# Recurrent mixer of a four-layer block: second head group prepared inside the first group's levels

## The chip, the cores and the metric

One core of a Trainium2 chip runs the whole program. The metric is the device time of one execution in microseconds, here the median of the runs shown.

## The reference, cut to what matters

The program computes four transformer layers on 256 tokens of width 1024 in float32. Each layer is a SwiGLU feed-forward part, a mixer and another feed-forward part, each with an adaptive norm before it. The mixer of the first layer is the recurrent one:

```python
q, fz, i, g = jnp.split(h @ w_in, 4, axis=-1)
q = jax.nn.silu(q)
f = jax.nn.sigmoid(fz)          # lb is zero here: one such layer
logf, k = jnp.log(f), 1.0 - f
b = jnp.cumsum(lf_c, axis=2)    # inside a chunk of 64 tokens, per head and channel
att = einsum('bhtk,bhsk,bhtsk->bhts', q_c, k_c, exp(b_t - b_s) where s <= t)
new_state = exp(b_last) * state + einsum(k_c * exp(b_last - b), v_c)
o = rmsnorm(inter + intra, onorm_g) * jax.nn.silu(g)
return o @ w_out
```

There are 8 heads of 128 channels.

## The kernel before, in words

**Pieces.** Every weight matrix goes through the engines in pieces of 128 x 2048 floats (1 MB). SyncE loads a piece into one of three slots of `raw` with two transfers (L335 to 343), after the piece three before it has been split. ScalarE copies it, rounded, to `wH` (`cut`, L491 to 496), VectorE subtracts to get the rest, `wL` (`cut`, L806 to 810), and TensorE multiplies with three products (high by high, low by high, high by low). The copies have three slots as well: ScalarE's `cut` of a piece waits until TensorE has "eaten" the piece three before it (`s_eaten`). All engines have their own program, in a fixed order written out by hand, and meet only through semaphores.

**The mixer's input projection** has 16 pieces, two for each 512 columns of `a_w_in`. Numbered from 0 in the order before: v first half (0, 1), forget of head group 0 (2, 3), query of group 0 (4, 5), v second half (6, 7), g first half (8, 9), g second half (10, 11), forget of group 1 (12, 13), query of group 1 (14, 15). The output projection `a_w_out` has pieces 16 to 19. v and g are laid out by token (`by_token`, L1519, TensorE's L1399, L1401, L1403), forget and query by channel (`by_channel`, L1533, lines L1543, L1545, L1546). They land in the PSUM halves `GUf` and `PAf`; the halves `PBf` and `TMf` take the gram products.

**A head group** is four heads. Its preparation: ScalarE takes a sigmoid and an absolute value of the forget columns (L613, L614), VectorE a minimum (L1022); ScalarE a sigmoid of the query (L618), VectorE the product (L1026); ScalarE the softplus by exp and ln (L622, L623), VectorE a subtraction and a scan over the tokens (L1032, L1033). Then nine levels, n = 0 to 8. In level n VectorE writes the exponents of level n + 1 (`exponents`, L979 to 989), ScalarE takes the exponential (L632), VectorE multiplies q and k in (`decayed`, L997, L998), TensorE makes 8 gram products (L1579; the last level 4, L1581), and VectorE selects that level's part of them into the table `att` (`select`, L1005, L1008, L1010). Behind the last level TensorE multiplies the table with v (12 products, L1598 to 1601), ScalarE squares (L584), VectorE sums and normalizes (L956, L961), multiplies with the norm's weights and with g (L1050, L1053), TensorE turns the heads (L1612), ScalarE writes the high part of the result (L602) and VectorE the low part (L967).

**Order before.** Group 0's levels run with one projection piece in each of levels 0 to 7, pieces 8 to 15. Then the output norm of group 0, its turn and low part, then group 1's preparation, then group 1's levels, with the cuts of pieces 16 and 17 near their end. The projections of pieces 16 and 17 (they need group 0 alone) run while VectorE normalizes group 1; then the turn of group 1, cuts of 18 and 19, and their projections. The next phase is a feed-forward part. Its first pieces come through the same ring, and pieces of the adaptive weights go through the buffer `ada` of two slots (`load_ada`, L378 to 384).

Of the kernel before, what the change touches and what calls it, by code (L numbers as in the profile page):

```python
# [22 lines left out]
ALU = mybir.AluOpType  # L23
# [78 lines left out]
def build(nc, T, out, upto=99):  # L102

    with ExitStack() as ctx:
# [56 lines left out]
        k_, q_, b_ = (M[:, n * D:(n + 1) * D] for n in range(3))  # L161
        E = [M[:, n * D:(n + 1) * D] for n in (3, 4, 5)]
        att = M[:, 6 * D:7 * D].rearrange("p (h s) -> p h s", s=P)
        attX = M[:, 7 * D:7 * D + 512].rearrange("p (h s) -> p h s", s=P)
# [167 lines left out]
        def _(sp):  # L332
# [63 lines left out]
            def ffn(l, j):  # L396
# [91 lines left out]
        def _(act):  # L488
# [115 lines left out]
            def hgrn():  # L604
# [5 lines left out]
                for grp in range(2):  # L610
                    forget, query = (GUf, PAf) if grp else (PAf, GUf)
                    act.wait_ge(s_eaten, t.next("done", 2))
                    act.activation(k_, forget, ACT.Sigmoid, scale=-1.0)  # L613
                    act.activation(E[0], forget, ACT.Abs).then_inc(s_key, 1)  # L614
                    if grp == 0:
                        cut()
                    act.wait_ge(s_eaten, t.next("done", 2))
                    act.activation(E[1], query, ACT.Sigmoid).then_inc(s_sigq, 1)  # L618
                    if grp == 0:
                        cut()  # L620
                    act.wait_ge(s_key, t.next(s_key))
                    chained(act.activation(E[0], E[0], ACT.Exp, scale=-1.0))  # L622
                    act.activation(E[0], E[0], ACT.Ln, bias=1.0).then_inc(s_ln, 1)  # L623
                    if grp == 0:
# [3 lines left out]
                    for n in range(9):  # L628
                        if n < 8:
                            act.wait_ge(s_expo, t.next(s_expo))  # L630
                            e = E[(n + 1) % 3]
                            act.activation(e, e, ACT.Exp).then_inc(s_decay, 1)  # L632
                        if grp == 0 and n < 6 or grp == 1 and n in (6, 8):
                            cut()
                        if grp == 0 and n == 3:
                            evacuate(g_[:, :, 0:512], GU[:, :, :], ACT.Silu)
                        if grp == 0 and n == 5:
                            evacuate(g_[:, :, 512:D], PY[:, 0:2, :], ACT.Silu)
                    head_norm(TMf, E[0])
                    head_root(8)  # L640
                    high_out(xH[:, 4 * grp:4 * grp + 4, :].rearrange("p d s -> p (d s)"), GUf if grp else PBf)
                cut()
                cut()
# [154 lines left out]
        def _(dve):  # L798
# [170 lines left out]
            def exponents(n, e):  # L969
# [3 lines left out]
                if n < 8:  # L973
                    m = 1 << (n - 1)
                    b4, e4 = (a.rearrange("p (g two m) -> p g two m", two=2, m=m) for a in (b_, e))
# [8 lines left out]
                b4, e4 = (a.rearrange("p (h c m) -> p h c m", h=4, c=4) for a in (b_, e))  # L984
# [7 lines left out]
            def decayed(n, e):  # L992
# [3 lines left out]
                e4, q4, k4 = (a.rearrange("p (g two m) -> p g two m", two=2, m=m) for a in (e, q_, k_))  # L996
# [3 lines left out]
            def select(n):  # L1000
# [3 lines left out]
                if n == 0:  # L1004
                    ins = dve.tensor_tensor(att, src, bc(ident.unsqueeze(1), [P, 8, P]), ALU.mult)  # L1005
                elif n < 8:
                    mask = cst[:, C_LEVEL + (n - 1) * P:C_LEVEL + n * P].bitcast(I32)
                    ins = dve.copy_predicated(att, bc(mask.unsqueeze(1), [P, 8, P]), src)  # L1008
                else:
                    ins = dve.tensor_copy(attX, src[:, 0:4, :])  # L1010
# [3 lines left out]
            def hgrn():  # L1014
# [4 lines left out]
                for grp in range(2):  # L1019
                    forget, query = (GUf, PAf) if grp else (PAf, GUf)  # L1020
                    dve.wait_ge(s_key, t.next(s_key))
                    dve.tensor_scalar(b_, forget, 0.0, None, ALU.min).then_inc(s_readD, 1)  # L1022
                    if grp == 0:
                        cut()
                    dve.wait_ge(s_sigq, t.next(s_sigq))
                    dve.tensor_tensor(q_, E[1], query, ALU.mult).then_inc(s_readD, 1)  # L1026
                    dve.wait_ge(s_readD, t.next(s_readD, 2))
                    if grp == 0:
                        cut()

                    dve.wait_ge(s_ln, t.next(s_ln))
                    chained(dve.tensor_tensor(E[1], b_, E[0], ALU.subtract))  # L1032
                    chained(dve.tensor_tensor_scan(b_, cst[:, C_SCAN:C_SCAN + 4 * S], E[1], 0.0, ALU.mult, ALU.add))  # L1033
                    if grp == 0:
                        cut()
                        cut()
                    for n in range(9):
                        if n < 8:
                            exponents(n + 1, E[(n + 1) % 3])
                        if n:  # L1040
                            decayed(n, E[n % 3])
                            select(n - 1)
# [878 lines left out]
```

## Time and profile before

| what | value |
|---|---|
| three runs | 2619.49, 2624.07, 2625.35 us; median 2624.07 |
| span of the profiled execution | 2623.9 us (its own time is not listed apart from the span) |
| TensorE matmuls busy | 2425.2 us, 92% |
| VectorE busy | 1732.2 us, 66% |
| ScalarE busy | 1097.4 us, 42% |
| recurrent mixer in the span | about 297 to 495 us |

Times in the views are microseconds from the span's start. PE is TensorE, DVE is VectorE, ACT is ScalarE, SPq is SyncE's queue. In the windows a row gives for each engine busy time and number of instructions, and behind them the granted TensorE clock (1.00 is full), the share of the DMA engines and GB/s. In the timeline a row ends with the idle time before the instruction and what released it. In the chain a row is a start, a length and what the end of the program hung on in that time.

### The profile page before, as it was taken

To read this page: it belongs to the slowest core of one execution; us is meant where nothing else is said; L and a number is where in the kernel's file an instruction comes from. 1 tells how busy PE (TensorE), PEld (TensorE's weight loads), DVE (VectorE), ACT (ScalarE), POOL (GpSimd) and SP (SyncE) were. 2 spreads that over 40 slices of the span, in tenths; PEclk is the share of its full clock that TensorE was granted. 3 is DMA by queue.
4 is the path that set the end of the run, shared out by engine and by line. 5 is a ranking of instruction groups with operands and counts; after the bars stand their busy time and mean duration, and the time that the engine had idled before them with its cause. 6 is when DMAs were issued, how large, how long until landed. Compare 5 with 4: busy or idle time off the path is not lost.

```text
span 2623.9 us, 32924 instructions
## 1 busy us (share of the span) xinstructions
PE 2425.2 (92%) x11906; PEld 2043.9 (78%) x11906; DVE 1732.2 (66%) x2090; ACT 1097.4 (42%) x1220; POOL 0.2 (0%) x4
## 2 busy tenths in 40 slices
PE   8999994899999995999999898999999989899998
PEld 8788884788788773788788796778878878777886
DVE  4777576687587785677687644568757764455444
ACT  1443543434433454433534334544343333463443
POOL 0000000000000000000000000000000000000000
PEclk9999997999999995999999987999999998898999
DMA  9788440498588640498498832248858892324553
GB/s 336 253 302 274 152 137 8 138 319 265 193 296 293 217 164 29 147 314 271 164 320 294 228 117 85 97 160 301 275 193 282 294 277 94 113 81 129 176 185 111
DMA packets 349089, 530.28 MB, mean 202 GB/s; under 512 B 14833, under 2 KB 208465, under 8 KB 348881
## 3 DMA queue, kind: packets, MB, share of 16 engines
q1 hardware_dynamic: 349008, 529.18, 60.6%
q8 instruction: 54, 0.88, 0.1%
q14 instruction: 27, 0.21, 0.0%
HBM read 528.08 MB, written 1.05 MB: 202 GB/s over the span
## 4 chain that ended last, share of the span: by engine, by line
PE 78%; DVE 12%; ACT 5%; issue 2%; SPq 2%; DMA 1%; DVEq 0%; ACTq 0%
PE GU L1399 12%; PE GU L1403 12%; PE GU L1401 12%; PE PY L1399 9%; PE PY L1401 9%; PE PY L1403 8%; DVE wL L810 3%; ACT wH L496 2%; PE TM L1473 2%; PE PY L1417 2%; PE GU L1485 2%; DVE acc L839 1%; PE TM L1449 1%; PE PY L1729 1%; PE PY L1627 1%
## 5 line engine op out<-in xcount | busy, mean ns | idle before, releaser
L810 DVE TENSOR_TENSOR wL<-raw,wH 128x2048 fp32r<-128x2048 f32 x352 | 794.5, 2279 | 308.7 <-ACT wH L496 308.0
L496 ACT ACTIVATE wH<-raw 128x2048 fp32r<-128x2048 f32 x352 | 659.5, 1899 | 223.1 <-PE PY L1403 101.4
L1399 PE MATMUL GU<-wH,xH 128*128 128x512 f32 (+1 forms) x1600 | 634.4, 397 | 28.3 <-issue 11.6
L1403 PE MATMUL GU<-wH,xL 128*128 128x512 f32 (+1 forms) x1600 | 623.2, 390 | 0.0
L1401 PE MATMUL GU<-wL,xH 128*128 128x512 f32 (+1 forms) x1600 | 622.5, 389 | 0.0
L1399 PEld LDWEIGHTS GU<-wH,xH 128*128 128x128 f32 x1600 | 302.5, 189 | 93.6 <-issue 29.4
L554 ACT ACTIVATE hH<-TM 128x512 fp32r<-128x512 f32 x88 | 52.6, 598 | 747.1 <-PE TM L1449 747.1
L839 DVE SCALAR_TENSOR_TENSOR acc<-ada,cs,acc 128x512 f32<-128x512 f32 x448 | 336.9, 752 | 23.1 <-DVE acc L839 2.6
L1403 PEld LDWEIGHTS GU<-wH,xL 128*128 128x128 f32 x1600 | 301.9, 189 | 63.5
L1401 PEld LDWEIGHTS GU<-wL,xH 128*128 128x128 f32 x1600 | 302.5, 189 | 58.3
L1399 PE MATMUL PY<-wH,hH 128*128 128x512 f32 x704 | 226.7, 403 | 26.2 <-DVE hL L920 24.8
L1401 PE MATMUL PY<-wL,hH 128*128 128x512 f32 x704 | 220.2, 394 | 0.0
L1403 PE MATMUL PY<-wH,hL 128*128 128x512 f32 x704 | 218.4, 392 | 0.0
L920 DVE TENSOR_TENSOR hL<-TM,hH 128x512 fp32r<-128x512 f32 x88 | 60.9, 692 | 234.7 <-ACT hH L554 231.2
L1399 PE MATMUL PY<-wH,xH 128*128 128x512 f32 x432 | 177.4, 411 | 8.3 <-DVE wL L810 6.9
L1401 PE MATMUL PY<-wL,xH 128*128 128x512 f32 x432 | 173.3, 401 | 0.0
L1403 PE MATMUL PY<-wH,xL 128*128 128x512 f32 x432 | 173.0, 401 | 0.0
L1399 PEld LDWEIGHTS PY<-wH,hH 128*128 128x128 f32 x704 | 128.1, 190 | 50.9 <-DVE wL L810 18.2
L1401 PEld LDWEIGHTS PY<-wL,hH 128*128 128x128 f32 x704 | 133.2, 189 | 30.0
L1403 PEld LDWEIGHTS PY<-wH,hL 128*128 128x128 f32 x704 | 133.3, 189 | 29.7
L1399 PEld LDWEIGHTS PY<-wH,xH 128*128 128x128 f32 x432 | 85.0, 197 | 30.3 <-issue 8.6
L550 ACT ACTIVATE sh<-GU 128x512 f32<-128x512 f32 x88 | 52.7, 598 | 118.2 <-PE GU L1403 118.2
(295 smaller groups left out, 2324.5 us busy)
## 6 DMA issues: line engine op xcount, KB each, us to landing
ada<-in_ada_w SPq DMA_DIRECT2D x128, 1024.0 KB, 7.5
raw<-in_ffn_wi SPq DMA_DIRECT2D x176, 512.0 KB, 6.0
raw<-in_ffn_w_in SPq DMA_DIRECT2D x176, 512.0 KB, 5.6
raw<-in_ffn_wo SPq DMA_DIRECT2D x88, 512.0 KB, 4.4
raw<-in_ffn_w_out SPq DMA_DIRECT2D x88, 512.0 KB, 4.4
raw<-in_mix_w_in SPq DMA_DIRECT2D x64, 512.0 KB, 4.8
M<-in_ada_w SPq DMA_DIRECT2D x16, 1024.0 KB, 8.5
raw<-in_a_w_in SPq DMA_DIRECT2D x32, 512.0 KB, 4.7
```

Source lines behind the costliest of these rows:

```text
L496: act.activation(wH[:, slot, 0:words], raw[:, slot, 0:words], ACT.Copy).then_inc(s_high, 1)
L550: act.activation(sh[:, 0, :, :], GU[:, :, 0:CF], ACT.Silu).then_inc(s_silu, 1)
L554: act.activation(hH[:, :, :].rearrange("p f s -> p (f s)"), TM[:, 0, :], ACT.Copy).then_inc(s_hh, 1)
L810: dve.tensor_tensor(wL[:, slot, 0:words], raw[:, slot, 0:words], wH[:, slot, 0:words], ALU.subtract).then_inc(s_split, 1)
L839: ins = dve.scalar_tensor_tensor(acc[:, :], w, c, acc[:, :], ALU.mult, ALU.add)
L920: dve.tensor_tensor(hL[:, :, :].rearrange("p f s -> p (f s)"), TM[:, 0, :], hH[:, :, :].rearrange("p f s -> p (f s)"), ALU.subtract).then_ ...
L1399: pe.matmul(outs[i], aH, wh[i], start=first, stop=False)
L1401: pe.matmul(outs[i], aH, wl[i], start=False, stop=False)
L1403: ins = pe.matmul(outs[i], aL, wh[i], start=False, stop=last)
L1417: ins = pe.matmul(PT[:, i, d, :], x[:, i, d * P:(d + 1) * P], diag[:, i, :], start=True, stop=True)
L1473: ins = pe.matmul(bank[:, k:k + 1], acc[:, k * P:(k + 1) * P], ones[:, :], start=fresh, stop=True, skip_group_check=not fresh)
L1485: ins = pe.matmul(GU[:, c % 2, n:n + 1], w, cs[:, 4 * q + k:4 * q + k + 1], start=(q == 0 and k == tiles[0] and n == 0), stop=False, skip_ ...
```

## The change

The group 1 tables `k_`, `q_`, `b_` and the log of the forget gate get places of their own in the buffer `ada`, which is free during the mixer, and `att`, `attX` of group 1 in `xn`. With this group 1 can be prepared while group 0's levels run. Norm scratch moves from `E[0]` to `shf`. Every `decayed`, `exponents`, `select` is the same instruction as before.

- The pieces are loaded in another order: v first half (0, 1), forget 0 (2, 3), query 0 (4, 5), forget 1 (6, 7), query 1 (8, 9), g first half (10, 11), v second half (12, 13), g second half (14, 15), then `a_w_out` (16 to 19).
- TensorE multiplies pieces 6 and 7 ahead of the levels, 8 and 9 in levels 0 and 1 of group 0, 10 and 11 in its levels 3 and 4; 12 and 13 in levels 0 and 1 of group 1, 14 and 15 in its levels 3 and 4. Output products of group 0 go to `GU`, directly ahead of gram 0 of group 1. Group 0's heads are turned in level 5 of group 1.
- ScalarE and VectorE do group 1's forget in level 1 of group 0, its query, softplus and scan in level 3. Cuts are made in levels 0, 1, 2, 3, 4 and 5 of group 0 and in 0, 1, 4 and 5 of group 1. The norm of group 0 is in level 1 of group 1, its high and low part in level 6. Piece 19 is cut behind the norm of group 1.
- SyncE waits, in the next feed-forward part, for the second turn of heads before it loads adaptive weights into `ada`.

The core of the diff:

```diff
+                        if with_ada and (l, j) == (0, 2):
+                            sp.wait_ge(s_ot, 2)
                         if with_ada:
                             load_ada(la, c0 + i, 0)
...
-                    for lo in (2 * D, D, 0, 2 * D + 512, 3 * D, 3 * D + 512, D + 512, 512):
+                    for lo in (2 * D, D, 0, D + 512, 512, 3 * D, 2 * D + 512, 3 * D + 512):
...
+                # ScalarE
+                forget(0, E[0])
+                cut()
+                query(E[1])
+                cut()
+                softplus(E[0])
+                cut()
+                for n in range(8):
+                    decay(n)
+                    if n < 3:
+                        cut()
+                    if n == 1:
+                        forget(1, lf_[1])
+                    if n == 3:
+                        query(q_[1])
+                        softplus(lf_[1])
+                        cut()
+                    if n == 4:
+                        cut()
+                    if n == 5:
+                        evacuate(g_[:, :, 0:512], PY[:, 0:2, :], ACT.Silu)
+                        cut()
+                for n in range(8):
+                    decay(n)
+                    if n == 0:
+                        cut()
+                    if n == 1:
+                        head_norm(GUf, shf)
+                        head_root(8)
                         cut()
                         evacuate(v_[:, :, 512:D], PY[:, 0:2, :])
...
+                    if n == 4:
+                        cut()
+                    if n == 5:
+                        evacuate(g_[:, :, 512:D], PY[:, 0:2, :], ACT.Silu)
+                        cut()
+                    if n == 6:
+                        high_out(xH[:, 0:4, :].rearrange("p d s -> p (d s)"), GUf)
+                head_norm(TMf, shf)
+                head_root(8)
+                cut()
+                high_out(xH[:, 4:8, :].rearrange("p d s -> p (d s)"), GUf)
...
+                # VectorE
+                forget(0)
+                cut()
+                query(0, E[1])
+                cut()
+                log_decay(0, E[0], E[1])
+                cut()
+                for n in range(9):
+                    level(0, n)
+                    if n < 3:
+                        cut()
+                    if n == 1:
+                        forget(1)
+                    if n == 3:
+                        query(1, q_[1])
+                        log_decay(1, lf_[1], lf_[1])
+                        cut()
+                    if n == 4 or n == 5:
+                        cut()
+                select(0, 8)
+                for n in range(9):
+                    level(1, n)
+                    if n == 0:
+                        cut()
+                    if n == 1:
+                        normed(0, GUf)
+                        cut()
+                    if n == 4 or n == 5:
+                        cut()
+                    if n == 6:
+                        low(0)
+                select(1, 8)
+                normed(1, TMf)
+                cut()
+                low(1)
...
+                # TensorE
+                by_channel(PAf, 0)
+                by_channel(PAf, 1)
...
+                pe.wait_ge(s_readD, t.next(s_readD))
+                for n in range(9):
+                    gram(0, n)
+                    if n < 2:
+                        by_channel(GUf, n)
+                    if n == 3:
+                        pe.wait_ge(s_readD, t.next(s_readD))
+                        by_token(B, 0)
+                    if n == 4:
+                        by_token(B, 1)
+                pe.wait_ge(s_readD, t.next(s_readD))
+                outputs(0, GU)
+                for n in range(9):
+                    gram(1, n)
+                    if n == 0 or n == 3:
+                        pe.wait_ge(s_readA, t.next(s_readA))
+                        by_token(B, 0)
+                    if n == 1 or n == 4:
+                        by_token(B, 1)
+                    if n == 5:
+                        turn_heads(0)
+                outputs(1, TM)
+                pe.wait_ge(s_readA, t.next(s_readA))
+                pe.wait_ge(s_xl, t.next(s_xl))
+                project(0, 0)
+                project(0, 1)
+                turn_heads(1)
                 pe.wait_ge(s_xl, t.next(s_xl))
                 project(1, 0)
                 project(1, 1)
```

Here `level(grp, n)` is `exponents` of n + 1, `decayed` of n and `select` of n - 1, and `log_decay` is the subtraction and the scan.

## Rows read from the trace of the kernel before

**Rows 1.** The page: its head and the busy times.

```profile
span 2623.9 us, 32924 instructions
PE 2425.2 (92%) x11906; PEld 2043.9 (78%) x11906; DVE 1732.2 (66%) x2090; ACT 1097.4 (42%) x1220; POOL 0.2 (0%) x4
```

**Rows 2.** The windows by stages of the mixer.

```profile
331.00:398.00 67.00, 60.91 (x413) 56.53 (x412) 47.84 (x51) 29.14 (x23) 0.00 (x0) 0.95 0.38 126
...
398.00:426.00 28.00, 10.08 (x61) 9.00 (x59) 13.35 (x13) 13.64 (x13) 0.00 (x0) 0.65 0.00 1
...
426.00:460.00 34.00, 18.11 (x121) 16.49 (x121) 32.73 (x45) 12.06 (x10) 0.00 (x0) 0.85 0.08 24
```

**Rows 3.** The chain of waits: gram products inside group 0's levels.

```profile
344.42 3.79 PE TM L1579 x16
...
353.87 1.78 PE PY L1579 x16
...
361.12 1.79 PE TM L1579 x16
```

**Rows 4.** VectorE's timeline: cuts, norm, low part, scan, ends of group 1's levels.

```profile
331.04 4.49 DVE L810 TENSOR_TENSOR wL<-raw,wH 128x2048 fp32r<-128x2048 f32 x2
...
399.49 0.69 DVE L1010 COPY M<-PY 128x512 f32<-128x512 f32 x1 [5.38 <-PE PY L1581]
404.35 1.22 DVE L956 TENSOR_REDUCE st<-M 128x8 f32<-128x1024 f32 x1 [4.16 <-ACT M L584]
...
408.80 1.22 DVE L1053 TENSOR_TENSOR M<-M 128x1024 f32<-128x1024 f32 x1
413.14 1.23 DVE L967 TENSOR_TENSOR xL<-PY,xH 128x1024 fp32r<-128x1024 f32 x1 [3.12 <-ACT xH L602]
...
423.37 2.29 DVE L1033 TENSOR_TENSOR_SCAN M<-cst,M 128x1024 f32<-128x1024 f32 x1
425.69 0.69 DVE L979 TENSOR_TENSOR M<-M 128x512 f32<-128x512 f32 x1
...
453.78 2.29 DVE L810 TENSOR_TENSOR wL<-raw,wH 128x2048 fp32r<-128x2048 f32 x1
...
459.20 0.69 DVE L1010 COPY M<-PY 128x512 f32<-128x512 f32 x1 [0.72 <-PE PY L1581]
```

**Rows 5.** ScalarE's timeline: a cut, then table loads and softplus of group 0.

```profile
320.76 1.91 ACT L496 ACTIVATE wH<-raw 128x2048 fp32r<-128x2048 f32 x1
322.69 1.28 ACT L622 ACT_TABLE_LOAD   x1
...
326.36 1.06 ACT L623 ACTIVATE M<-M 128x1024 f32<-128x1024 f32 x1
```

**Rows 6.** The windows: granted clock around TensorE's idle stretches.

```profile
342.00:344.00 2.00, 0.00 (x0) 0.00 (x0) 2.00 (x4) 0.81 (x1) 0.00 (x0) 0.50 0.44 71
...
404.00:408.00 4.00, 0.00 (x0) 0.00 (x0) 3.28 (x5) 1.74 (x3) 0.00 (x0) 0.81 0.00 0
...
434.00:438.00 4.00, 2.31 (x21) 2.12 (x20) 3.96 (x6) 1.06 (x1) 0.00 (x0) 1.00 0.00 0
...
460.00:464.00 4.00, 4.00 (x19) 4.00 (x20) 2.22 (x1) 0.00 (x0) 0.00 (x0) 0.50 0.26 86
```

**Rows 7.** The chain of waits: group 0's outputs done, then group 1's, to the next phase.

```profile
403.22 1.03 ACT M L584
...
459.95 0.80 PE TM L1598 x2
...
475.98 0.89 PE GU L1612 x8
...
482.18 0.77 PE PY L1399
...
489.33 1.93 ACT wH L496
```

**Rows 8.** The page: the mixer's weight loads, size and time to landing.

```profile
raw<-in_a_w_in SPq DMA_DIRECT2D x32, 512.0 KB, 4.7
```

More of the change, by code:

```diff
@@ L609, in hgrn, with forget @@
                 cut()
-                for grp in range(2):
-                    forget, query = (GUf, PAf) if grp else (PAf, GUf)
+                def forget(grp, e):
                     act.wait_ge(s_eaten, t.next("done", 2))
-                    act.activation(k_, forget, ACT.Sigmoid, scale=-1.0)
-                    act.activation(E[0], forget, ACT.Abs).then_inc(s_key, 1)
-                    if grp == 0:
-                        cut()
-                    act.wait_ge(s_eaten, t.next("done", 2))
-                    act.activation(E[1], query, ACT.Sigmoid).then_inc(s_sigq, 1)
-                    if grp == 0:
+                    act.activation(k_[grp], PAf, ACT.Sigmoid, scale=-1.0)
+                    act.activation(e, PAf, ACT.Abs).then_inc(s_key, 1)
@@ new lines, in query, with softplus, decay @@
+                def query(e):
+                    act.wait_ge(s_eaten, t.next("done", 2))
+                    act.activation(e, GUf, ACT.Sigmoid).then_inc(s_sigq, 1)
+                def softplus(e):
+                    act.wait_ge(s_key, t.next(s_key))
+                    chained(act.activation(e, e, ACT.Exp, scale=-1.0))
+                    act.activation(e, e, ACT.Ln, bias=1.0).then_inc(s_ln, 1)
+                def decay(n):
+                    act.wait_ge(s_expo, t.next(s_expo))
+                    e = E[(n + 1) % 3]
+                    act.activation(e, e, ACT.Exp).then_inc(s_decay, 1)
@@ L626, in hgrn @@
                         cut()
                         evacuate(v_[:, :, 512:D], PY[:, 0:2, :])
[L628 to L638, printed above, removed]
@@ L967, in low_out, with exponents @@
                 dve.tensor_tensor(dst, src, high, ALU.subtract).then_inc(s_xl, 1)
-            def exponents(n, e):
+            def exponents(grp, n, e):
                 if n < 8:
                     m = 1 << (n - 1)
-                    b4, e4 = (a.rearrange("p (g two m) -> p g two m", two=2, m=m) for a in (b_, e))
+                    b4, e4 = (a.rearrange("p (g two m) -> p g two m", two=2, m=m) for a in (b_[grp], e))
                     shape = [P, 4 * S // (2 * m), m]
@@ L983, in exponents @@
                     return
[L984 removed]
+                b4, e4 = (a.rearrange("p (h c m) -> p h c m", h=4, c=4) for a in (b_[grp], e))
                 chained(dve.tensor_tensor(e4[:, :, 0:2, :], bc(b4[:, :, 0:2, 63:64], [P, 4, 2, 64]), b4[:, :, 0:2, :],
@@ L1018, in hgrn, with forget, query @@
                 cut()
-                for grp in range(2):
-                    forget, query = (GUf, PAf) if grp else (PAf, GUf)
+                def forget(grp):
                     dve.wait_ge(s_key, t.next(s_key))
-                    dve.tensor_scalar(b_, forget, 0.0, None, ALU.min).then_inc(s_readD, 1)
-                    if grp == 0:
-                        cut()
+                    dve.tensor_scalar(b_[grp], PAf, 0.0, None, ALU.min).then_inc(s_readD, 1)
+                def query(grp, e):
@@ L1033, in hgrn @@
[L1033 to L1042, printed above, removed]
-                        if grp == 0 and n < 6 or grp == 1 and n == 7:
-                            cut()
@@ L1555, in hgrn @@
                 norm_and_first()
-                A, B = [GU[:, i, :] for i in range(NT)], [PY[:, i, :] for i in range(NT)]
+                B = [PY[:, i, :] for i in range(NT)]
                 by_channel(PAf, 0)
@@ new lines, in hgrn, with gram @@
+                by_channel(PAf, 0)
+                by_channel(PAf, 1)
+                def gram(grp, n):
+                    if n:
+                        pe.wait_ge(s_z, t.next(s_z))
+                    if n > 1:
+                        pe.wait_ge(s_sel, t.next(s_sel))
+                    dst = (PBf if n % 2 == 0 else TMf).rearrange("p (h s) -> p h s", s=P)
+                    e = E[n % 3].rearrange("p (h s) -> p h s", s=P)
+                    kk, qq = (e, e) if n else (a[grp].rearrange("p (h s) -> p h s", s=P) for a in (k_, q_))
+                    for h in range(8 if n < 8 else 4):
+                        if n < 8:
+                            ins = pe.matmul(dst[:, h, :], kk[:, h, :], qq[:, h, :], start=True, stop=True)
+                        else:
+                            ins = pe.matmul(dst[:, h, :], kk[:, 2 * h, :], qq[:, 2 * h + 1, :], start=True, stop=True)
+                    ins.then_inc(s_gram, 1)
@@ L1595, in hgrn, with outputs @@
+                def outputs(grp, banks):
                     pe.wait_ge(s_sel, t.next(s_sel, 2))
```

109 lines of the change are left out of this document (35 added, 74 removed).

## The prediction

> **What bounds the kernel now.** The page comes first: TensorE works over 92% of the span, VectorE over 66% [rows 1]. These shares mix four layers; the change touches only the recurrent mixer, from about 297 to 495 us. So the second view is the windows by its stages [rows 2]. The reader is to see three regimes. From 331 to 398 (levels of head group 0) TensorE works 61 of 67 us. From 398 to 426 (tail of group 0, preparation of group 1) no engine works more than half the time. From 426 to 460 (levels of group 1) VectorE works 32.7 of 34 us. The third view, the chain of waits, confirms it: a group 0 level takes 7.24 us (353.87 to 361.12) on TensorE, 1.79 of gram products and 5.45 of a by-token piece [rows 3]; the nine levels of group 1 take 34.2 us of VectorE with one cut among them (425.69 to 459.89) [rows 4].
>
> **The change, part by part.** No arithmetic is added or taken: the same pieces, products and passes. Three things move. (a) Projection pieces: group 1's forget and query pieces come forward, v's second half and both g halves go back; group 0's levels then carry four pieces and not eight, group 1's four and not none. (b) Group 1's forget, query, softplus and scan run inside levels 1 and 3 of group 0. (c) Group 0's output norm and its low part run inside levels 1 and 6 of group 1. So the hole between the last gram selection of group 0 (ends 400.2) and the first exponents of group 1 (425.69) goes: 25.5 us [rows 4].
>
> What takes its place, by VectorE's in-order queue, from 331.04, where the first scan ends. Work: the levels of one group are 31.0 us (425.69 to 459.89, less the 2.29 of a cut and 0.9 of waits), twice 62.0; eleven cuts of about 2.25, 24.8; forget, query and subtraction of group 1, each one pass over 1024 floats like the low part of 1.23, and the scan of 2.29, together 6.0; norm of group 0 from 404.35 to 410.02, 5.7, and a low part of 1.23 [rows 4]. Sum 99.7, which would end group 1 at 430.7 and not 459.9, 29 us earlier. That holds only if VectorE never waits. The waits, each found by laying the new order out with the durations of the rows:
>
> In group 0: 2.9 us before the second cut of its levels (exponential, then ScalarE's cut of 1.91, now one behind the other) [rows 5]. Two sigmoid passes, each behind a table load of 1.28, leave about 1.0 each. Softplus of group 1 takes ScalarE 4.73 us (322.69 to 327.42) [rows 5], of which 1.2 lies beside the query product: 3.5. In level 5, ScalarE is told to wait for g's first half (Silu) before it cuts: the piece behind gram 4 starts only when VectorE has done the exponents of level 4 behind softplus and scan, about 372.4, and with grams at the low clock 3.4 and the piece 6.0 it is eaten at 382; Silu 1.03 and cut 1.91 follow, so VectorE, ready at 380.1, waits 4.8. Some 0.8 for late grams. Sum 14, so group 0 ends at about 399, one us before today. Group 0 carries less TensorE work but no less time: its cover is gone to VectorE's queue.
>
> In group 1: the cut of piece 15 (g, second half of the rows) sits right behind exponents of level 0. It may be written only when piece 12 (v, second half) is eaten, since the ring has three slots, and TensorE eats piece 12 only after the twelve output products of group 0 and gram 0 of group 1: 3.0 (400.2 to 403.22 now) + 1.8 + 5.45, from 399.1 to 409.4 [rows 3, 7]. ScalarE's cut ends at 411.3; VectorE was ready at 400.2 and stands 11 us. Behind the standing instruction are all of level 1, and with it gram 1, and with gram 1 the next piece. So the same wait comes back smaller: cut of piece 16 waits for piece 13 (eaten about 425.5; VectorE ready at 423.0 after the norm): 4.5. Piece 17 waits for 14: 4.6. Piece 18 waits for 15, with Silu ahead: 2.8. Sum 23. Group 1 ends at about 430.7 + 14 + 23 = 468, 8 us later than now.
>
> The tail. Now: from 459.95 to 475.98 run the outputs and two projection pieces, which at 5.45 each leave 5.1 for the outputs at the low clock; then the turn 0.9, then high part 1.02, the cut of piece 18 (1.91 and 2.29), and the third projection piece, from 482.18, half of it at the low clock, is eaten at 489.3 [rows 7]: 29.3 in all, and from there the next phase starts through a cut. After: piece 18 is cut long before, so the cut goes out of the path and low part (1.23) comes in: 5.1 + 10.9 + 0.9 + 1.1 + 1.3 + 5.45 = 24.8, with 0.3 of hops 25.1. This gives back 4.2. The wait added to SyncE's queue before the next phase's adaptive weights (until the second turn of heads, about 485) costs nothing: today the next pieces of the ring come ahead of it in the queue and the cut before the next phase is at 489.33 [rows 7]; it is issued about then, with the next pieces behind it in the queue not earlier either. The mixer's own loads are the same 32 transfers in another order; each is issued when the piece three before it is split and lands in 4.7 us [rows 8], over 7 us before its cut is due in the new order: nothing. Group 1's tables lie in other buffers, in passes of the same shape: nothing either.
>
> **Sum**: 8.2 − 4.2 = +4. The nearest bounds: TensorE at full clock through the outputs gives 2.1 back (3.0 for 5.1); at the low clock through every late block it costs more (rival 1). The tail's third piece may or may not meet the low clock, 1.4. I take +3.5, as one of the two may fall well: 2623.9 + 3.5 = 2627.4. The span and the median of the runs shown (2624.07) differ by 0.2, so the sum stands for both. What a measurement of this kernel can tell from no change is about 0.2%, 5 us.
>
> A rule that bears on the sum stands in the clock. The rows: TensorE's granted clock stood at 0.50 in 342 to 344, while it waited for VectorE, and a gram from 344.42 ran slow; it fell again within 404 to 408 with TensorE idle, was 1.00 at 434 to 438 and 0.50 through the outputs at 460 to 464 [rows 3, 6]. A gram at 0.50 (1.2 GHz) takes 3.79 and not 1.79 [rows 3]. The sum takes the low level where TensorE stood over 5 us before a block, and full clock for outputs and piece 12.
>
> The Trainium skill ("TensorE: Matmul & The Clock Gate", HAM oscillation) says that idle gaps between bursts put TensorE back to half rate and that each new burst then starts cold; it advises to keep the work contiguous. By that rule this change, which breaks eight contiguous pieces into short bursts, is worse than my sum: rival 1, priced below from the rows.
>
> **Rivals.**
> 1. *Low clock at every late block: slower.* TensorE waits 3 to 7 us before nearly every gram of the new order. Where the next VectorE wait hangs on the block (outputs with piece 12, pieces 14 and 15, the third projection piece), a cold start costs 2.1, 2.2, 2.2 and 1.4 (a block of gram and piece was 9.45 cold, 344.42 to 353.87, against 7.24) [rows 3]: +7.9 on the forecast, so 2635.3. For it: the outputs of 460 to 464, cold behind sparse grams. Against: at 434 to 438 the same sparse grams ran at 1.00 [rows 6].
> 2. *The wait at the group boundary does not bite: faster.* If piece 12 were eaten by the time VectorE comes to cut 15, 11 us go and 2627.4 becomes 2616.4. It decides at whether waits of VectorE from 331 to the end of group 1 sum to under 33 (29 less work time plus 4 of tail); I have 37. For it: 25.5 us of hole do go, and my waits are a layout. Against: the piece stands behind the outputs in TensorE's order, and the cut ahead of level 1 in both other queues.
> 3. *It moves work and no time: none.* Group 0 is paced by VectorE as long as it was by TensorE, and group 1 stretches by as much as the hole held: 0, 2624. It is where the forecast goes if two or three small waits fall away; near it, only the mechanism is the same.
>
> **Chances.** Forecast 0.50 (its own range 2622 to 2633), rival 1 0.22, rival 2 0.16, rival 3 0.12. Slower by over 0.2% is all of rival 1 and a third of the forecast: 0.38. Faster by over 0.2%: rival 2 and a little: 0.17. Within: 0.45. The range leaves out the outer parts of rivals 1 and 2: 2615 to 2638.
>
> **What would show it.** Right: no hole between group 0's last selection and group 1's first exponents; group 1's levels take near 68 us, VectorE's longest wait is on ScalarE's cut right after its first exponents, about 11 us, with ScalarE waiting on TensorE's by-token piece; group 0's levels still end near 399; the third projection piece starts 2 to 3 us after the turn, with no cut before it. Each of the 4 us waits should be found on a cut in levels 1, 4 and 5. Wrong: VectorE busy over 85% from 400 to 460 (rival 2), or granted clock under 0.7 over the group 1 levels (rival 1).

## The result and the profile after

| | before | after |
|---|---|---|
| median, 20 runs each | 2623.84 us | 2631.31 us |
| lowest to highest | 2619.49 to 2627.72 | 2623.61 to 2633.86 |
| ratio, with its 95% interval | | 1.0023 [1.0017, 1.0029] |
| span of the profiled execution | 2623.9 us | 2627.2 us |
| mixer, from one norm's gate copy to the next | 218.8 us | 224.6 us |

The change makes the program about 6 us slower (0.23% of 2624; the two medians of 20 runs differ by 7.5), where +3.5 with the range 2615 to 2638 was forecast. The last row is read from ScalarE's copies of the gate (292.45 and 511.25 before, 293.00 and 517.56 after), which enclose the mixer's part of the trace. It shows +5.8 us. That the spans differ by only 3.3 comes from the later phases, in which nothing is changed; so the mixer's row is the one that the runs agree with. The gate copy stands behind the next norm, so that stretch takes in a little of the next phase too.

The head of the page after the change:

```profile
span 2627.2 us, 32931 instructions
PE 2429.1 (92%) x11906; PEld 2048.5 (78%) x11906; DVE 1732.4 (66%) x2090; ACT 1101.0 (42%) x1223; POOL 0.2 (0%) x4
```

The work is the same [rows 1]: as many matmuls, as many VectorE instructions, three more on ScalarE (table loads). So all of the time is in waits and in the clock. The same stages by windows, 332 to 399 for the levels of group 0 and 399 to 472 for those of group 1 (which were 426 to 460 before [rows 2]):

```profile
332.00:399.00 67.00, 47.60 (x279) 43.42 (x277) 51.55 (x54) 35.67 (x28) 0.00 (x0) 0.82 0.32 110
...
399.00:472.00 73.00, 50.76 (x264) 44.95 (x264) 46.29 (x55) 25.12 (x21) 0.00 (x0) 0.79 0.18 58
```

The columns are those of [rows 2]: the third number from the end is the granted clock. VectorE works 46.3 of 73 us in group 1's levels, where it was at 32.7 of 34 before. TensorE no longer fills group 0's levels (47.6 of 67 and not 60.9), and those take as long as before. The hole of 25.5 us is gone, and its time is back in small pieces. VectorE's timeline shows them, with the wait at the end of the row [rows 4]:

```profile
385.78 2.29 DVE L840 TENSOR_TENSOR wL<-raw,wH 128x2048 fp32r<-128x2048 f32 x1 [4.92 <-ACT wH L499]
...
398.47 0.69 DVE L1040 COPY M<-PY 128x512 f32<-128x512 f32 x1
399.20 0.69 DVE L1009 TENSOR_TENSOR M<-ada 128x512 f32<-128x512 f32 x1
399.81 0.69 DVE L1012 TENSOR_TENSOR M<-ada 128x512 f32<-128x512 f32 x1
411.54 2.29 DVE L840 TENSOR_TENSOR wL<-raw,wH 128x2048 fp32r<-128x2048 f32 x1 [11.04 <-ACT wH L499]
...
428.55 2.29 DVE L840 TENSOR_TENSOR wL<-raw,wH 128x2048 fp32r<-128x2048 f32 x1 [5.46 <-ACT wH L499]
...
447.61 2.29 DVE L840 TENSOR_TENSOR wL<-raw,wH 128x2048 fp32r<-128x2048 f32 x1 [5.37 <-ACT wH L499]
...
456.44 2.29 DVE L840 TENSOR_TENSOR wL<-raw,wH 128x2048 fp32r<-128x2048 f32 x1 [2.89 <-ACT wH L499]
...
470.12 1.33 DVE L1038 COPY_PREDICATED xn<-cst,TM 128x1024 f32<-128x1024 int32 x1 [1.12 <-PE TM L1636]
```

Group 1 begins 0.04 us behind the last selection of group 0 (399.16 to 399.20). Then VectorE stands 11.04 us before the cut of piece 15, and before each of the three cuts behind it. ScalarE's timeline tells what it stood for:

```profile
400.53 1.06 ACT L631 ACTIVATE M<-M 128x1024 f32<-128x1024 f32 x1 [6.03 <-DVE M L1012]
409.60 1.91 ACT L499 ACTIVATE wH<-raw 128x2048 fp32r<-128x2048 f32 x1 [8.01 <-PE PY L1463]
...
426.60 1.91 ACT L499 ACTIVATE wH<-raw 128x2048 fp32r<-128x2048 f32 x1 [7.52 <-PE PY L1463]
```

The exponential ends at 401.6, the cut may start only at 409.6: until then TensorE makes the outputs, gram 0 of group 1 and piece 12. That is the ring of three slots: the copy of piece 15 goes where piece 12 still lies.

### The profile page after: what moved, and what is told of

Same layout as the page of the kernel before. It is cut to its first block, busy times and chain, and to the rows that moved or that the text cites. A ratio compares the mean times of both kernels' runs of the same rounds, so it can differ in the third digit from the quotient of the medians.

```text
span 2627.2 us, 32931 instructions
## 1 busy us (share of the span) xinstructions
PE 2429.1 (92%) x11906; PEld 2048.5 (78%) x11906; DVE 1732.4 (66%) x2090; ACT 1101.0 (42%) x1223; POOL 0.2 (0%) x4
## 4 chain that ended last, share of the span: by engine, by line
PE 77%; DVE 12%; ACT 6%; issue 3%; DMA 1%; SPq 1%; DVEq 0%; ACTq 0%
PE GU L1459 12%; PE GU L1463 12%; PE GU L1461 12%; PE PY L1459 9%; PE PY L1461 9%; PE PY L1463 9%; DVE wL L840 3%; ACT wH L499 3%; PE TM L1533 2%; PE GU L1545 2%; DVE acc L869 1%; PE PY L1477 1%; PE TM L1509 1%; PE PY L1802 1%; PE PY L1700 1%
## 5 line engine op out<-in xcount | busy, mean ns | idle before, releaser
L1459 PE MATMUL GU<-wH,xH 128*128 128x512 f32 (+1 forms) x1584 | 628.0, 396 | 28.9 <-issue 11.6
L1459 PE MATMUL PY<-wH,hH 128*128 128x512 f32 x704 | 226.6, 403 | 25.3 <-DVE hL L950 23.9
L950 DVE TENSOR_TENSOR hL<-TM,hH 128x512 fp32r<-128x512 f32 x88 | 60.9, 692 | 236.9 <-ACT hH L557 234.0
L1459 PE MATMUL PY<-wH,xH 128*128 128x512 f32 x448 | 184.5, 412 | 5.3 <-DVE xL L997 2.4
L1461 PE MATMUL PY<-wL,xH 128*128 128x512 f32 x448 | 180.1, 402 | 0.0
L1463 PE MATMUL PY<-wH,xL 128*128 128x512 f32 x448 | 179.3, 400 | 0.0
L1463 PEld LDWEIGHTS PY<-wH,xL 128*128 128x128 f32 x448 | 87.5, 195 | 19.4
```

Source lines behind the costliest of these rows:

```text
L950: dve.tensor_tensor(hL[:, :, :].rearrange("p f s -> p (f s)"), TM[:, 0, :], hH[:, :, :].rearrange("p f s -> p (f s)"), ALU.subtract).then_ ...
L1459: pe.matmul(outs[i], aH, wh[i], start=first, stop=False)
L1461: pe.matmul(outs[i], aH, wl[i], start=False, stop=False)
L1463: ins = pe.matmul(outs[i], aL, wh[i], start=False, stop=last)
```

## The experiments

Each kernel was timed against the kernel before on the same chip. "Mixer" is again the stretch between the two gate copies of its profile: 218.8 us before, 224.6 with the change. "To the end of group 1" is its part up to VectorE's last selection: 167.4 us before. What is left is the tail and the next norm.

| run | ratio to before | interval | to the end of group 1, us | mixer, us |
|---|---|---|---|---|
| the change | 1.0023 | 1.0017 to 1.0029 | 179.2 | 224.6 |
| cut 15 later | 0.9968 | 0.9955 to 0.998 | 166.6 | 211.0 |
| piece 12 early | 0.998 | 0.9971 to 0.999 | 172.3 | 217.7 |
| scan at the boundary | 1.0014 | 1.0005 to 1.0023 | 178.8 | 226.6 |
| group 0 laid out anew | 0.9976 | 0.9967 to 0.9985 | 165.1 | 212.8 |
| filler in the tail | 1.0015 | 1.0006 to 1.0024 | 178.5 | 222.3 |
| fillers in group 1 | 1.0015 | 1.0006 to 1.0024 | 176.0 | 221.4 |
| both groups anew | 0.9914 | 0.9902 to 0.9927 | 147.4 | 192.8 |
| the same and filler | 0.99 | 0.9887 to 0.9914 | 147.3 | 191.1 |
| the same, two cuts ahead | 0.9886 | 0.9871 to 0.9901 | 142.4 | 186.8 |

The two columns of microseconds come from one profiled execution each, and part of a mixer's length is not the edit's doing. Where nothing was edited, the stretch from the last cut before the next norm to the gate copy took 18.7 us with the change, 19.4 in the run with cut 15 later and 21.1 in two others, by where TensorE met the low clock in it (granted 0.50 from 509 to 512.6 in one of the two, 1.00 with the change); and the end of group 0 came 105.6 to 106.4 us behind the gate copy in four kernels that are the same up to there. So a difference of 1 us between two profiles tells little, and one of 2 us only where it is found at the edited place.

### The wait at the group boundary

ScalarE, and VectorE likewise:

```diff
                 for n in range(8):
                     decay(n)
-                    if n == 0:
-                        cut()
                     if n == 1:
                         head_norm(GUf, shf)
                         head_root(8)
                         cut()
+                    if n == 2:
                         evacuate(v_[:, :, 512:D], PY[:, 0:2, :])
+                        cut()
```

> The changed kernel with the cut of piece 15 moved from level 0 of group 1 to behind the norm of group 0 in level 1, and the cut of piece 16 to level 2. Ring theory (the cut at the group boundary makes VectorE stand until TensorE has eaten piece 12, 11.0 us in the changed kernel's trace): VectorE starts level 1 at once and does the norm in that time; the cut of 15 finds its slot free, the cut of 16 waits 2 to 3 us for piece 13. Laid out with the durations of the trace, the cut of 16 ends near 422 and not 430.8 with level 2 behind it and not ahead, so group 1 ends 12 us earlier: ratio to before about 1.0023 - 0.0046 = 0.998, 2618 us. Low-clock theory (the time goes into TensorE's cold starts, VectorE's stand is only where it shows): moving a cut leaves the gaps of TensorE as they are, so little goes: under 3 us, ratio about 1.001 to 1.002.

(On ScalarE the copy of v's second half moves along, out of level 1 into level 2.) Measured: 0.9968, 13.6 us off the mixer, 12.6 of them by the end of group 1, where 12 were expected. The part between the groups, by VectorE's timeline of that run:

```profile
397.29 0.69 DVE L1040 COPY M<-PY 128x512 f32<-128x512 f32 x1
...
402.87 1.23 DVE L1035 TENSOR_TENSOR xn<-PY,cst 128x1024 f32<-128x1024 f32 x1 [1.13 <-PE PY L1636]
...
410.35 2.29 DVE L840 TENSOR_TENSOR wL<-raw,wH 128x2048 fp32r<-128x2048 f32 x1 [0.54 <-ACT wH L499]
...
418.52 2.29 DVE L840 TENSOR_TENSOR wL<-raw,wH 128x2048 fp32r<-128x2048 f32 x1 [2.20 <-ACT wH L499]
...
434.69 2.29 DVE L840 TENSOR_TENSOR wL<-raw,wH 128x2048 fp32r<-128x2048 f32 x1 [6.25 <-ACT wH L499]
```

The 11.04 us are down to 0.54, because level 1 and the norm now lie ahead of the cut. The cut of piece 16 waits 2.20, as expected; that of piece 17 waits 6.25 for 5.37. Two cuts moved in two queues turn the slower kernel into one 0.3% faster than before. The low-clock theory allowed 3 us and falls as the main cause. This run alone would not quite settle it, since with TensorE at work all through 399 to 412 its clock stayed up behind:

```profile
412.00:420.00 8.00, 5.34 (x32) 4.56 (x30) 5.80 (x7) 3.88 (x3) 0.00 (x0) 1.00 0.39 131
```

With the change it was 0.50 there. What the clock is worth by itself the fillers in group 1 show below: 3.2 us.

The condition of the prediction's faster rival was tried by itself: TensorE multiplies piece 12 in level 5 of group 0.

```diff
                     if n == 4:
                         by_token(B, 1)
+                    if n == 5:
+                        pe.wait_ge(s_readA, t.next(s_readA))
+                        by_token(B, 0)
...
-                    if n == 0 or n == 3:
+                    if n == 3:
```

> The changed kernel with TensorE's product of piece 12 moved from behind the outputs of group 0 (level 0 of group 1) into level 5 of group 0, where TensorE idles; cuts stay. This is the condition of the prediction's faster rival: piece 12 eaten before VectorE comes to cut 15. Ring theory: the 11.0 us wait shrinks to the 3 us that ScalarE's cut takes behind the exponential; piece 13 is eaten near 415.5 and cut 16 ends at about 420 and not 430.8: 11 us earlier, ratio 0.998 to 0.999, about 2619 us. If the prediction's price for the rival is wrong because the waits behind it grow instead (each later cut waits for the piece three before it, and those hang on VectorE, not on piece 12), the gain is under 5 us: ratio about 1.0005 or more. Low-clock theory: the extra work in level 5 keeps the clock up for the grams of levels 6 to 8, a gain of 1 to 2 us there in addition.

Measured: 0.998, which against 1.0023 is the 11 us expected. Its one profile shows less: the mixer is only 6.9 us shorter. That profile is of the slowest of the nine runs (2625.77 us, median 2621.24), so the two need not agree. The wait at the boundary went from 11.04 to 2.92, which is 8.1; the end of group 0 came 1.2 later, with a wait of 1.20 for a gram behind the added piece. The wait behind the boundary stayed:

```profile
404.79 2.29 DVE L840 TENSOR_TENSOR wL<-raw,wH 128x2048 fp32r<-128x2048 f32 x1 [2.92 <-ACT wH L499]
...
421.82 2.29 DVE L840 TENSOR_TENSOR wL<-raw,wH 128x2048 fp32r<-128x2048 f32 x1 [5.47 <-ACT wH L499]
```

So the rival's condition was what the change lacked, and its price of 11 us is what the runs show, where the profile shows 7. The extra 1 to 2 us that the low-clock theory promised don't show in that profile.

### What paces group 0

```diff
                     if n == 3:
                         query(1, q_[1])
-                        log_decay(1, lf_[1], lf_[1])
                         cut()
...
                 select(0, 8)
+                log_decay(1, lf_[1], lf_[1])
```

> The changed kernel with group 1's subtraction and scan on VectorE moved out of level 3 of group 0 to the boundary between the groups; ScalarE's softplus stays in level 3. Theory that group 0's levels are as long as before because VectorE's in-order queue waits there for softplus (3.5 us) and does the scan (3.6 us): group 0 ends 7 us earlier, and at the boundary the 3.6 us of scan lie inside the 11 us wait for piece 12, so all 7 us are kept: ratio about 0.9996, 2623 us. If the wait for g's first half in level 5 (4.9 us) is what paces group 0, the 7 us come back there and the ratio stays at 1.002.

Measured: 1.0014, where 0.9996 was expected for 7 us: 2 us at the likeliest, and the intervals of this run and of the change overlap. The expectation fell; of its two readings the second, that the time comes back, is the nearer one. The profile's mixer is even 2.1 us longer than with the change, but that is no effect of the scan: to the end of group 1 it is 0.4 shorter, and 2.2 are lost in the next norm, whose second turned tokens VectorE waits for 3.43 us and not 1.25. (This profile is of the slowest of the eleven runs.) Why group 0 gains nothing stands in VectorE's timeline:

```profile
366.76 2.29 DVE L840 TENSOR_TENSOR wL<-raw,wH 128x2048 fp32r<-128x2048 f32 x1 [5.32 <-ACT wH L499]
...
384.74 2.29 DVE L840 TENSOR_TENSOR wL<-raw,wH 128x2048 fp32r<-128x2048 f32 x1 [5.55 <-ACT wH L499]
...
398.77 0.69 DVE L1040 COPY M<-PY 128x512 f32<-128x512 f32 x1
```

VectorE no longer waits for softplus by name, but its cut behind it does, since ScalarE makes softplus first. It comes 1.7 us earlier (366.76 for 368.45), the cut of piece 14 only 1.0, and group 0 ends at 399.5, as with the change (399.2). What has to move is what stands in ScalarE's queue ahead of a cut:

```diff
                 softplus(E[0])
                 cut()
+                cut()
                 for n in range(8):
                     decay(n)
-                    if n < 3:
+                    if n == 0:
                         cut()
                     if n == 1:
                         forget(1, lf_[1])
-                    if n == 3:
+                    if n == 2:
+                        cut()
                         query(q_[1])
                         softplus(lf_[1])
+                    if n == 3:
                         cut()
                     if n == 4:
                         cut()
-                    if n == 5:
                         evacuate(g_[:, :, 0:512], PY[:, 0:2, :], ACT.Silu)
+                    if n == 5:
                         cut()
```

TensorE multiplies pieces 10 and 11 one level earlier, in levels 2 and 3.

> The changed kernel with group 0's levels laid out anew and group 1 left alone: ScalarE cuts piece 9 ahead of the first exponential, does query and softplus of group 1 in level 2 (VectorE still takes them in level 3), cuts piece 13 ahead of g's first half, in level 4, and piece 14 in level 5; TensorE multiplies pieces 10 and 11 in levels 2 and 3. In the scan-at-boundary run the wait for softplus only turned into a wait for the cut behind it (5.3 us), so the theory is now: group 0 is paced by what stands in ScalarE's queue ahead of each cut, not by VectorE's work. Laid out with the trace's durations, the waits of 2.9, 3.5 and 4.9 us go and group 0 ends near 386.5 and not 399.2, 12 to 13 us earlier; the 11 us at the boundary stay: ratio about 0.9975, 2618 us. Rival: the time of group 0 is VectorE's own work and TensorE at the low clock; then under 4 us go: ratio 1.001 or more.

Measured: 0.9976, 11.8 us off the mixer and 14.1 to the end of group 1 (the next norm, 21.1 us here, takes 2.3 back). The boundary wait is as it was, and its cut 13.4 us earlier (0.3 of that is a shift between the traces):

```profile
398.17 2.29 DVE L843 TENSOR_TENSOR wL<-raw,wH 128x2048 fp32r<-128x2048 f32 x1 [11.04 <-ACT wH L499]
```

(411.54 with the change.) So group 0's waits of 2.9, 3.5 and 4.9 us, 11.3 together, are worth what they measure, and the rival that allowed 4 us falls. The run moves them all at once and does not tell them apart.

### The low clock

```diff
                 turn_heads(1)
+                for _ in range(20):
+                    pe.transpose(TM[:, 0, 0:P], ident, ident)
                 pe.wait_ge(s_xl, t.next(s_xl))
```

> The changed kernel with 20 transposes of the identity into a free bank between the second turn of heads and the third projection piece (2.2 us of work that nothing needs, in a gap of 2.4 us). In the changed kernel's trace this piece took 7.3 us (489.36 to 496.7) where one at full clock takes 5.5: the clock falls just after it has begun. If the gap ahead is what drops it, the piece now takes 5.5 us and the mixer is 1.5 to 1.9 us shorter (ratio about 1.0016). If the clock falls anyway, or the fillers come late and push the piece back, nothing or up to 0.5 us worse.

The windows with the change, where the third projection piece starts at 489.36, behind a gap of 2.37 us:

```profile
488.00:490.00 2.00, 0.65 (x3) 0.56 (x4) 1.35 (x2) 1.84 (x2) 0.00 (x0) 1.00 1.11 363
490.00:494.00 4.00, 4.00 (x12) 3.12 (x11) 3.02 (x4) 0.00 (x0) 0.00 (x0) 0.57 0.75 258
```

and with the filler:

```profile
488.00:490.00 2.00, 1.81 (x10) 1.33 (x9) 1.43 (x2) 1.10 (x1) 0.00 (x0) 1.00 1.09 359
490.00:494.00 4.00, 4.00 (x20) 3.28 (x18) 2.27 (x4) 0.00 (x0) 0.00 (x0) 1.00 0.79 268
```

TensorE keeps its full clock, the window from 490 to 494 holds 20 matmuls and not 12, and the tail is 1.6 us shorter. The mixer is 2.3 us shorter and the ratio 1.0015; 0.7 of the 2.3 lie ahead of the filler, where nothing was edited, and the interval of the ratio overlaps the change's.

One run speaks against reading this as a rule of the gap. With cut 15 later the third piece began behind the same gap, without any filler (the first line is the change's, the second that run's, the third its window):

```profile
489.36 0.50 PE L1459 MATMUL PY<-wH,xH 128*128 128x512 f32 x1 [2.37 <-DVE xL L997]
```

```profile
476.11 0.50 PE L1459 MATMUL PY<-wH,xH 128*128 128x512 f32 x1 [2.37 <-DVE xL L997]
```

```profile
478.00:482.00 4.00, 4.00 (x19) 3.29 (x19) 1.77 (x4) 0.04 (x1) 0.00 (x0) 1.00 0.79 249
```

The clock stayed at 1.00 and the tail was as short as with the filler. Of the seven kernels with this gap of 2.37 us, six lost 1.6 us to the clock behind it and one did not; the three with the filler did not. Why the one escaped, no run here shows.

The same ahead of grams 1, 2 and 6 of group 1, into the gram's own bank:

```diff
+                    if grp == 1:
+                        for _ in range({1: 45, 2: 45, 6: 36}.get(n, 0)):
+                            pe.transpose(dst[:, 0, :], ident, ident)
                     if n:
                         pe.wait_ge(s_z, t.next(s_z))
```

> The changed kernel with idle transposes of the identity ahead of grams 1, 2 and 6 of group 1 (45, 45 and 36 of them, about 5, 5 and 4 us), into the gram's own bank, where TensorE otherwise stands 6.8, 6.8 and 5.5 us; nothing else moved. It measures the prediction's low-clock rival by itself. In the changed kernel's trace the granted clock is 0.5 from 412 to 420 and from 430 to 438 and from 460 to 468; with the fillers it should be 1.00 there, grams take 1.8 and not 3.8, and the block of gram 1 and piece 13 is 2 us shorter, that of grams 2, 3 and piece 14 up to 3 us, gram 7 no longer late by 1.1. Rival's price if it is the main term: 5 us or more (ratio 1.0000 or less). If only blocks that a cut waits for count, 3 to 5 us (1.0005 to 1.0012). If the fillers run into the grams that they precede, no gain.

Measured: the mixer 3.2 us shorter, all of it by the end of group 1, and the ratio 1.0015, whose interval overlaps the change's. The windows from 412 and from 430, with the change (granted clock in the third column from the end) and then with the fillers:

```profile
412.00:420.00 8.00, 3.71 (x17) 3.71 (x18) 7.62 (x10) 3.46 (x4) 0.00 (x0) 0.50 0.40 131
430.00:438.00 8.00, 4.70 (x20) 4.42 (x21) 7.86 (x11) 2.84 (x3) 0.00 (x0) 0.50 0.40 131
```

```profile
412.00:420.00 8.00, 6.12 (x50) 5.66 (x49) 7.46 (x10) 3.60 (x5) 0.00 (x0) 1.00 0.39 133
430.00:438.00 8.00, 4.92 (x37) 4.58 (x38) 7.93 (x12) 2.52 (x3) 0.00 (x0) 1.00 0.40 127
```

The clock is 1.00 through both, and yet only 3 us go: the cut of piece 16 waits 2.80 and not 5.46, that of piece 17 4.72 and not 5.37, the boundary 11.04 as before. Part of the expectation missed: from 460 to 468 the clock was 0.79 and not 1.00, and the gram that was late by 1.12 was late by 1.20.

```profile
412.17 2.29 DVE L840 TENSOR_TENSOR wL<-raw,wH 128x2048 fp32r<-128x2048 f32 x1 [11.04 <-ACT wH L499]
...
426.51 2.29 DVE L840 TENSOR_TENSOR wL<-raw,wH 128x2048 fp32r<-128x2048 f32 x1 [2.80 <-ACT wH L499]
...
444.76 2.29 DVE L840 TENSOR_TENSOR wL<-raw,wH 128x2048 fp32r<-128x2048 f32 x1 [4.72 <-ACT wH L499]
```

### Both groups laid out anew

Group 0's new order of above stays. TensorE multiplies pieces 12 and 13 in levels 4 and 5 of group 0, 14 and 15 in levels 0 and 1 of group 1, and turns group 0's heads in level 2. Piece 15 is cut in level 6 of group 0; 16, 17 and 18 in levels 0, 1 and 3 of group 1.

> The same, and pieces 12 and 13 multiplied in levels 4 and 5 of group 0 (v's second half evacuated in level 7), piece 15 cut in level 6 of group 0; in group 1 pieces 14 and 15 multiplied in levels 0 and 1, cuts of 16, 17, 18 in levels 0, 1 and 3, the turn in level 2, high and low part in level 4. Every cut then finds its slot free when VectorE comes. Ring theory: VectorE hardly waits any more and its work sets the end: group 0 ends near 389, group 1 near 434 and not 472: 35 to 38 us earlier than the changed kernel, ratio 0.987 to 0.989, 2591 to 2596 us, under both kernels. If other waits (TensorE's pieces late at the low clock, ScalarE's tables) take their place, half of it: 2605 to 2612 us.

> The kernel of the previous run with the 20 idle transposes between the second turn of heads and the third projection piece. If the low clock in that piece comes from the gap of 2.4 us alone, 1.5 to 2 us less than the previous run, as in the changed kernel; if the denser group 1 keeps the clock up by itself, no difference, or up to 0.3 us worse.

> The kernel of both groups laid out anew, with the filler, and two more cuts moved ahead on ScalarE: piece 16 ahead of group 1's first exponential, piece 18 into level 2, ahead of g's second half. In the profile of the kernel with both groups laid out anew VectorE still waits 2.9 us before each of these cuts. If ScalarE's order is all that makes it wait, 5 to 6 us go: ratio 0.988, 2592 to 2594 us by medians on the same chip. If the time returns as a wait for late grams, under 2 us.

Measured: 0.9914, 0.99 and 0.9886. The first stays short of its 0.989, with two waits that the layout had missed, each for a cut that stands in ScalarE's queue behind something else (the exponential, and g's second half):

```profile
393.55 2.29 DVE L844 TENSOR_TENSOR wL<-raw,wH 128x2048 fp32r<-128x2048 f32 x1 [2.92 <-ACT wH L499]
...
417.59 2.29 DVE L844 TENSOR_TENSOR wL<-raw,wH 128x2048 fp32r<-128x2048 f32 x1 [2.88 <-ACT wH L499]
```

The filler took 1.7 us off the mixer, 1.6 of them in the tail, though its effect on the ratio is inside the intervals. The last kernel moves those two cuts ahead:

```diff
+                cut()
                 for n in range(8):
                     decay(n)
-                    if n == 0:
-                        cut()
...
+                    if n == 2:
+                        cut()
                     if n == 3:
                         evacuate(g_[:, :, 512:D], PY[:, 0:2, :], ACT.Silu)
-                        cut()
```

Its mixer is 186.8 us long, 4.3 less, of the 5 to 6 expected (the intervals of these two ratios overlap, so the step is read from the profiles); the median is 2593.33 us, 1.1% under the kernel before on the same chip and under both kernels. VectorE's waits for ScalarE's cuts from 332 to 472 (total, number, longest), first with the change, then in this kernel, where that stretch holds the tail as well:

```profile
DVE wL L840 <- ACT wH L499: 34.4, 9, 11.0
```

```profile
DVE wL L844 <- ACT wH L499: 7.6, 7, 4.2
```

## Why the prediction was right, and where it was off

**What bounds and what goes.** Right. The hole of 25.5 us closed, and no arithmetic was added.

**Group 0.** Waits of 14 us were forecast. Those of VectorE's timeline sum to 15.1 (2.93, 0.66, 0.89, 0.53, 1.12, 3.52, 0.57, 4.92), and the group ends at 399.16 for "about 399". That hit is partly luck: by the prediction's own terms (331.04, 52.8 of work, 14 of waits) the group would end at 397.8, and on the clock of the trace before it ended at 398.6. The sentence that its cover is gone to VectorE's queue names the wrong queue for the waits: the scan run and the new order of group 0 together show that ScalarE's order ahead of the cuts makes them.

**The boundary.** Right to the tenth, 11.04 for 11, and shown to be the ring's wait by two runs, one that moves the cut and one that moves the product.

**The small waits behind it.** Here the size was off. 4.5, 4.6 and 2.8 were forecast, and 5.46, 5.37, 2.89 and a late gram of 1.12 measured: 26.2 with the boundary and a small one of 0.28, where the sum had 23. The blocks that these waits hang on ran colder than the rows that I took them from: gram 1 and piece 13 took 10.2 (416.30 to 426.5), where the cold block of the rows is 9.45, and gram 3, with no gap ahead of it, took 2.97 and not 1.79. Group 1 ends at 472.2, or 471.6 on the clock of the trace before (the mixer begins 0.55 later), and not at 468 (which by its own terms is 430.7 + 37 = 467.7).

**The tail.** 25.1 us forecast, 24.6 measured (472.17 to 496.80), but by two errors that cancel: the outputs ran at full clock (3.0 and not 5.1), and the third piece met the low clock, 7.4 us (489.36 to 496.80) and not 5.45, which the sum had left open at 1.4. Against 29.4 before, 4.8 come back for 4.2. The second of the two is the piece that stayed at full clock in another run, so this term could as well have come out 1.6 us lower.

**Sum.** 471.6 − 459.9 − 4.8 = +6.9 at the end of the third piece, of which the next norm gives 1.1 back: its turned tokens ran cold before and not after (windows at the end of this point). That is the +5.8 of the mixer, and the 6 us of the runs, for the forecast's 3.5 to 4. What was mis-sized is the term for the small waits: the two middle ones of group 1 short by 1.7 us together, the late gram of 1.1, 1.1 in group 0 and 0.4 of smaller ones, less 0.4 of work that the sum had too much: 3.9 of the 467.7 to 471.6.

```profile
498.00:502.00 4.00, 3.48 (x17) 3.21 (x17) 3.05 (x7) 2.13 (x3) 0.00 (x0) 0.58 0.71 281
```

```profile
505.00:509.00 4.00, 2.20 (x17) 2.04 (x18) 3.28 (x8) 3.20 (x6) 0.00 (x0) 1.00 0.11 43
```

(Windows over the first turned tokens of the next norm, before and after.)

**The rivals.** The low clock was priced at 7.9 us in addition. The fillers in group 1 take out 3.2 us and the filler in the tail 1.6, so by the profiles it is a real term of some 5 us if they add up (they were not run together on this kernel, and their ratios do not stand clear of the change's), and a part of it was in my sum already. The median of 2631.3 lies as far above the forecast (2627.4) as below this rival (2635.3), so the time alone could not choose between them; the waits do. Its sign, a granted clock under 0.7 over group 1's levels, did not come: it was 0.79. Behind gaps of 6.80 us the granted clock was 0.50, in 412 to 420 and in 430 to 438. This agrees with the rule of the Trainium skill ("TensorE: Matmul & The Clock Gate", HAM oscillation), that each burst behind a gap starts cold; it did not decide the case, since 13 us hung on one cut. The third piece, behind its shorter gap of 2.37 us, began at full speed. The wait that does not bite needed piece 12 eaten early, which the change does not do; made so, it gave 11 us by the runs and 7 by the profile, for a price of 11. Its sign, VectorE busy over 85%, did not come either (46.3 of 73 us). The rival of no change is outside the interval.

**The wait on SyncE's queue** cost nothing that shows: the first adaptive piece was issued at 487.25, right behind the second turn, for 485.66 before, and the next phase's ring went on. No run leaves this wait out.

## What to carry to other kernels

In a ring with in-order queues, the place of a copy in each queue can be worth as much as the work that is moved: ask of every copy which product frees its slot, and put it behind the work that needs neither. When a stage is spread over another, lay the waits out one by one; the total of busy time promised 29 us here, and of two orders of the same work one lost 6 us and the other, with 20 idle transposes added, won 30. Look for the pacing queue one step further back than the engine that waits: taking softplus out of VectorE's wait did nothing until ScalarE's order changed. And before a microsecond between two profiles is put down to an edit, look for the place where it arises.

## What was not expected of the hardware

Behind a gap of 2.37 us before the third piece the clock fell, and it fell about 1 us after TensorE had begun again: the first product from 489.36 came at full speed, and those from 490.5 to 493.5 took 0.63 and not 0.39 us. The kernel with both groups laid out anew shows the same (first product at 457.32, 0.63 us from 458.8). The gap does not decide it, though: with cut 15 later the same gap of 2.37 us was followed by 0.39 us throughout. With idle transposes in the gap the clock stood at 1.00 there in all three kernels that have them. Whether such a filler costs anything elsewhere, no run here shows.
